# Four channel norms of part two: VectorE adds the squares, TensorE sums them into a token column

## The reference, cut to what matters

```python
def rmsnorm(x, g):
    xf = x.astype(jnp.float32)
    y = xf * lax.rsqrt(jnp.mean(xf * xf, axis=-1, keepdims=True) + EPS)
    return (y * g.astype(jnp.float32)).astype(x.dtype)

# layer 0: h = h + ab_mixer(rmsnorm(h, g0), ...)   gated delta rule and windowed attention
#          h = h + mlp(rmsnorm(h, m0))             relu squared, 1024 -> 4096 -> 1024
# layer 1: h = h + c_mixer(rmsnorm(h, g1), ...)    dense attention over 528 tokens
#          h = h + mlp(rmsnorm(h, m1))
```

## Time and profile before

| what | value |
|---|---|
| time, median of 3 runs | 3802.8 us (3795.65 to 3806.92) |
| profiled execution, first to last instruction | 3796.5 us |
| TensorE matmul busy | 2674.6 us, 70% of the span |
| VectorE busy | 2038.2 us, 54% |
| GpSimd busy | 1860.8 us, 49% |
| ScalarE busy | 802.5 us, 21% |
| mean granted TensorE clock | 0.851 |
| part two | from about 2021 us to the end |

### The profile page before, as it was taken

The page is one execution under the profiler, slowest core; times in us unless marked ns, Lnnn a source line. Parts: engine busy times, 40 slices in busy tenths (PEclk is TensorE's granted clock), DMA queues, the critical chain, the costliest instruction groups (busy, mean ns, idle before and its releaser), DMA issues.

```text
span 3796.5 us, 37057 instructions
## 1 busy us (share of the span) xinstructions
PE 2674.6 (70%) x14128; PEld 1994.0 (53%) x14128; DVE 2038.2 (54%) x4133; ACT 802.5 (21%) x1515; POOL 1860.8 (49%) x1389
## 2 busy tenths in 40 slices
PE   6521887207862277542776888888889998998999
PEld 3421444004431144211224777777789997777887
DVE  6599867888678877588443534544220103532010
ACT  2100111001110011111113322332332322443231
POOL 0166656775567756488761322222354543125463
PEclk8755999558886599776998987998999999999999
DMA  5388889897899879999991210000223332012332
GB/s 173 138 310 299 288 276 338 306 341 261 298 314 344 314 264 333 343 336 336 353 345 28 67 28 1 1 1 1 56 73 91 88 90 59 26 45 78 95 95 78
DMA packets 417970, 693.79 MB, mean 183 GB/s; under 512 B 35784, under 2 KB 280691, under 8 KB 417667
## 3 DMA queue, kind: packets, MB, share of 16 engines
q0 software_dynamic: 147456, 536.94, 39.7%
q1 hardware_dynamic: 270339, 154.50, 14.1%
HBM read 689.26 MB, written 2.10 MB: 182 GB/s over the span
## 4 chain that ended last, share of the span: by engine, by line
PE 51%; DVE 16%; POOL 12%; DMA 11%; issue 6%; ACT 3%; SPq 1%; DVEq 0%; ACTq 0%; POOLq 0%
PE PS L1601 25%; POOL ring L608 12%; DMA ring<-in_peer_v,eidx 7%; PE PS L775 7%; DMA ring<-in_peer_u,eidx 3%; DVE ring L1308 3%; PE PS L754 2%; PE PS L1502 1%; PE PS L1511 1%; PE PS L660 1%; PE PS L1508 1%; DVE W L1182 1%; PE PS L1611 1%; DVE X L1323 1%; PE PS L1623 1%
## 5 line engine op out<-in xcount | busy, mean ns | idle before, releaser
L608 POOL DMA_INDIRECT ring<-in_peer_u,eidx x512 | 630.7, 1232 | 409.1 <-DVE eidx L1285 175.9
L608 POOL DMA_INDIRECT ring<-in_peer_v,eidx x512 | 588.9, 1150 | 355.2 <-PE PS L775 215.4
L1601 PE MATMUL PS<-held_uH,GW 128*128 128x264 f32 (+1 forms) x3008 | 668.3, 316 | 35.4 <-POOL BIG_value L2128 31.3
L1308 DVE CUSTOM_DVE_ANT_0 ring<-ring,hn 128x1024 f32<-128x1024 f32 x512 | 615.7, 1224 | 117.9 <-DMA ring<-in_peer_u,eidx 110.8
L775 PE MATMUL PS<-ring,dg 128*128 128x512 f32 x1024 | 534.9, 662 | 168.7 <-DMA ring<-in_peer_v,eidx 164.4
L2114 POOL TENSOR_TENSOR GW<-held_wr,GW 128x1024 fp32r<-128x1024 f32 x178 | 428.9, 2411 | 449.5 <-ACT GW L1891 449.5
L1601 PEld LDWEIGHTS PS<-held_uH,GW 128*128 128x128 f32 x3008 | 504.2, 193 | 79.9 <-issue 34.1
L1601 PE MATMUL PS<-BIG_value,GW 128*128 128x264 f32 (+1 forms) x1504 | 448.1, 313 | 0.0
L775 PEld LDWEIGHTS PS<-ring,dg 128*128 128x128 f32 x1024 | 198.0, 208 | 460.8 <-DMA ring<-in_peer_v,eidx 281.3
L1323 DVE SCALAR_TENSOR_TENSOR X<-ring,gact,X 128x1024 f32<-128x1024 f32 x256 | 328.7, 1284 | 179.8 <-DMA ring<-in_peer_v,eidx 176.0
L1601 PE MATMUL PS<-hid,GW 128*128 128x264 f32 (+1 forms) x2304 | 368.6, 322 | 0.0
(11 more groups left out here) (465 smaller groups left out, 3581.1 us busy)
## 6 DMA issues: line engine op xcount, KB each, us to landing
held_wr<-in_w_ff SPq DMA_DIRECT2D x128, 512.0 KB, 4.1
wqr<-in_peer_wq SPq DMA_DIRECT2D x64, 512.0 KB, 8.0
held_wr<-in_w_in_ab SPq DMA_DIRECT2D x18, 512.0 KB, 3.7
ring<-in_peer_u,eidx POOLq DMA_INDIRECT x512, 6.2
ring<-in_peer_v,eidx POOLq DMA_INDIRECT x512, 6.0
BIG<-in_w_in SPq DMA_DIRECT2D x4, 1536.0 KB, 11.3
held_wr<-in_w_qkv_c SPq DMA_DIRECT2D x12, 512.0 KB, 3.9
w_out<-in_w_out SPq DMA_DIRECT2D x1, 4096.0 KB, 20.6
```

What stands on the lines that cost most here:

```text
L608: e.indirect_dma_start(out=ring[:, i % RING, :], out_offset=None, in_=rows_u if k < HK else rows_v, in_offset=bass.IndirectOffsetOnAxis(ap ...
L1308: e.tensor_tensor_reduce(row, row, hn[:, :], 1.0, 0.0, ALU.mult, ALU.add, act[:, k:k + 1]).then_inc(*n.up(e_dot))
L1601: ins = e.matmul(bank[b + a][:, 0:w], (hi, lo)[w_][:, k * P:(k + 1) * P], (x_hi, x_lo)[x_][:, c0:c0 + w], start=(first and w_ == 0 and x_ ...
```

## The change

It touches the four channel norms alone.

- VectorE adds the squares of tiles 0 to 6 into `R` (`add_square`): six adds of a full tile for each norm. The square of tile 7 stays in `sq[1]`.
- TensorE's `sums` calls for these norms go. In their place `norm` issues, behind the last gemm, short matmuls whose stationary operand is a slice of `R` and whose moving operand is one column of 1/1024 (`share`): 6 slices of 88 tokens in ALL, 4 of 128 in LATE. Each leaves the sum of its tokens as a column, token by partition. The same is done with `sq[1]`, into another bank.
- VectorE adds EPS to the first column block, and then adds the second; ScalarE takes the root, VectorE the reciprocal, all on 88 by 6 (or 128 by 4) values.
- TensorE spreads them back to rows by 6 (4) matmuls: stationary the column broadcast to 128, moving the identity. VectorE's multiply for `uT` then reads the inverse root from PSUM and not from `R`.

```diff
+    two["share"] = np.full((P, 1), 1.0 / D, f)
...
+    ALL, LATE = Span(0, 264, 2, 88), Span(META, 512, 1, P)
...
-        def norm(from_k, sp=ALL):
-            for k in range(from_k, 8):
-                sums(ones2, sq[k % 2], k == 0, k == 7, sp)
+        def norm(inverted, sp=ALL):
+            w = sp.few
+            for src, ready, at in ((R, nxt(n_acc, 6), 4), (sq[1], nxt(n_sq, 8), 5)):
+                e.wait_ge(*ready)
+                for i, c0 in enumerate(sp.cuts):
+                    ins = e.matmul(bank[at][0:w, 300 + i:301 + i], src[:, c0:c0 + w], share, start=True, stop=True)
+                ins.then_inc(*up(n_sum))
+            e.wait_ge(rinv, inverted)
+            for i in range(len(sp.cuts)):
+                ins = e.matmul(sp.row_sums(i), vec2[0:w, 98 + i:99 + i].to_broadcast([w, P]), ident2[0:w, 0:w], start=True, stop=True)
+            ins.then_inc(*up(n_sum))
             return normed()
...
             for m in range(8):
                 gemm(operands if m == 0 else [waited(o) for o in operands], h_res, sp)
-                if squares and m:
-                    sums(ones2, sq[(m - 1) % 2], m == 1, False)
...
+        def square_tile(k, sp=ALL):
+            if k >= 2:
+                e.wait_ge(n_acc, count["norm"] + max(k - 2, 1))
+            e.activation(sp.cut(sq[k % 2]), sp.cut(hT[:, k, :]), ACT.Square).then_inc(*up(n_sq))
...
-            d = sp.cut(R)
-            sqrt(e, n, d)
+            sqrt(e, n, vec2[0:sp.few, 98:98 + len(sp.cuts)])
...
+        def add_square(k, sp=ALL):
+            e.wait_ge(*nxt(n_sq, 2 if k == 1 else 1))
...
+                e.tensor_tensor(sp.cut(R), sp.cut(R), sp.cut(sq[k % 2]), ALU.add).then_inc(*up(n_acc))
...
         def norm(gcol, sp=ALL):
-            summed(8)
-            inverse((sp.two(R), sp.cut(R)), sp.pair(4), 1.0 / D)
+            summed()
+            part = lambda at: bank[at][0:sp.few, 300:300 + len(sp.cuts)]
+            few = vec2[0:sp.few, 98:98 + len(sp.cuts)]
+            e.tensor_scalar(few, part(4), EPS, None, ALU.add).then_inc(*up(dve))
+            e.wait_ge(*now(dve))
+            summed()
+            e.tensor_tensor(few, few, part(5), ALU.add).then_inc(*up(var))
+            e.wait_ge(*nxt(root))
+            e.reciprocal(few, few).then_inc(*up(rinv))
...
-                e.scalar_tensor_tensor(sp.cut(uT[:, k, :]), sp.cut(hT[:, k, :]), vec2[:, gcol + k:gcol + k + 1], sp.cut(R),
+                e.scalar_tensor_tensor(sp.two(uT[:, k, :]), sp.two(hT[:, k, :]), vec2[:, gcol + k:gcol + k + 1], sp.pair(4),
                                        ALU.mult, ALU.mult).then_inc(*up(n_u))
...
             for m in range(8):
                 b = output(units, sp)
+                if squares and m >= 2:
+                    add_square(m - 1, sp)
                 e.wait_ge(g_done, count["unit"])
```

More of the change, by code:

```diff
@@ L436, in emit, with __init__ @@
     class Span:
-        def __init__(self, c0, w, parts):
-            self.c0, self.w, self.parts = c0, w, parts
+        def __init__(self, c0, w, parts, few):
+            self.c0, self.w, self.parts, self.few = c0, w, parts, few
+            self.cuts = range(c0, c0 + w * parts, few)
             self.halves = [(c0 + w * a, w) for a in range(parts)]
@@ L456, in pair, with row_sums @@
             return PS[0:rows, b:b + self.parts, 0:self.w]
-    ALL, LATE = Span(0, 264, 2), Span(META, 512, 1)
+        def row_sums(self, i):
+            c = i * self.few
+            return PS[:, 4 + c // self.w, c % self.w:c % self.w + self.few]
+    ALL, LATE = Span(0, 264, 2, 88), Span(META, 512, 1, P)
     def row(m, width):
@@ L1630, in waited, with residual @@
             return [(hi, lo, None) for hi, lo, _ in operands]
-        def norm(from_k, sp=ALL):
-            for k in range(from_k, 8):
-                sums(ones2, sq[k % 2], k == 0, k == 7, sp)
+        def norm(inverted, sp=ALL):
[9 more added lines that the diff above has]
+            ins.then_inc(*up(n_sum))
             return normed()
-        def residual(operands, squares, sp=ALL):
+        def residual(operands, sp=ALL):
             for m in range(8):
                 gemm(operands if m == 0 else [waited(o) for o in operands], h_res, sp)
-                if squares and m:
-                    sums(ones2, sq[(m - 1) % 2], m == 1, False)
         def mlp(last):
             sp = LATE if last else ALL
-            ops = norm(7, sp)
+            ops = norm(INV_MLP1 if last else INV_MLP0, sp)
             for half in range(2):
@@ L1650, in mlp @@
                 hops = [(r(hid[:, 0, m, :]), r(hid[:, 1, m, :]), nxt(lo_g)) for m in range(16)]
-                residual([hops[0:8], hops[8:16]], half and not last, sp)
+                residual([hops[0:8], hops[8:16]], sp)
         e.wait_ge(t_hT, 2 * NB)
@@ L1657, in second_tensor @@
         e.transpose(bank[6][:, 0:97], vr2[0:97, :], ident2[0:97, 0:97]).then_inc(*up(s_vecp))
-        ops = norm(0)
+        ops = norm(INV_NORM0)
         e.wait_ge(n_w16, 2)
@@ L1730, in second_tensor @@
         yops = [(r(uH[:, k, :]), r(uL[:, k, :]), nxt(lo_g if (k < 4) == (k % 2 == 1) else lo_v)) for k in range(8)]
-        residual([yops], True)
+        residual([yops])
         mlp(False)
-        ops = norm(7)
+        ops = norm(INV_C)
         def rope(m):
@@ L1797, in second_tensor @@
         yops = [(r(uH[:, h, :]), r(uL[:, h, :]), nxt(lo_g)) for h in range(8)]
[L1798 to L1802, removed]
+        residual([yops], LATE)
         mlp(True)
@@ L1882, in second_scalar @@
         up, now, nxt = n.up, n.now, n.next
-        count = {"split": 0, "unit": 0, "out": 0, "sq": 0}
+        count = {"split": 0, "unit": 0, "out": 0, "sq": 0, "norm": 0}
         limit = [BEFORE_DELTA]
@@ L2345, in mlp @@
                 lows[0] += 16
-                residual(2, sp)
+                residual(2, half and not last, sp)
         lows = [0]
@@ L2353, in second_vector @@
         e.wait_ge(*now(dve))
+        for k in range(1, 7):
+            add_square(k)
         norm(0)
@@ L2449, in second_vector @@
         lows[0] += 4
-        residual(1)
+        nxt(n_sq, 17)
+        residual(1, True)
         lows[0] += 4
@@ L2511, in second_vector @@
         lows[0] += 8
-        residual(1, LATE)
+        nxt(n_sq, 10)
+        residual(1, True, LATE)
         lows[0] += 4
```

19 lines of the change are left out of this document (16 added, 3 removed).

## The result

The changed kernel took 3776.2 us in the median of 20 runs (3749.2 to 3802.4), the kernel before 3801.5 on the same chip (20 runs): ratio 0.9931, interval 0.9916 to 0.9947, 20 to 32 us off. The forecast was 25 us off, to 3778. The profiled execution took 3777.2 us with a span of 3775.4; before, the span was 3796.5.

The account below looks back on a forecast made before the run. The prediction took TensorE, in part two nearly all its gemms, to bound the kernel. Its terms, 15.8 + 5.0 + 3.0 + 2.0 - 0.4 = 25.4 us off, put the median at 3778 us, range 3768 to 3788.

Parts of the forecast that it names:

- own signs: Last square to first multiply was to take near 3.6, 3.6 and 2.9 us in norms MLP0, C and MLP1.
- rival A: Norm chains: granted clock falls in the pause, short matmuls double (7.8 us), full gemms slow (6); 11.6 off, 3791; chance 0.11.
- Term 1: Three residuals feeding norms: six channel sums each, 0.89 or 0.86 us, no longer hold up the next gemm; 15.8 us off.
- Term 1's cover: VectorE's adds of squares, 0.7 to 2.2 us, fit inside the shortest gemm, 5.8 us, so nobody waits.
- Terms 2 and 3: Chains from last square to first multiply: 2.5 us off each in norms MLP0 and C, 3.0 in MLP1.
- Term 4: Norm AB, adds on the path and short matmuls at half pace: first multiply 2.0 us sooner, between 1 and 5.
- Term 5: VectorE's multiply reading the inverse root from PSUM costs 0.1 us a norm, 0.4 in all.
- Rivals B and C: B (0.05): something else held the gemm, 9.6 us off; C (0.02): short matmuls don't overlap weight loads, 3812 or 3832 us.
- The sum: All gains less the PSUM cost: 15.8 + 5.0 + 3.0 + 2.0 - 0.4 = 25.4 us off, bounds 22.4 to 30.2.

Follow-up runs that it names:

- Fillers and wide slices together: Changed kernel plus unread matmuls in TensorE's norm-chain pauses and slices streaming their one column 64 times; ratio to the kernel before 0.9903, repeated 0.9915.
- fillers alone: Changed kernel plus float32 matmuls that nothing reads in TensorE's norm-chain pauses, slices still of one column; ratio to the kernel before 0.9897.
- wide slices alone: Changed kernel with every slice's matmul streaming its one column 64 times, pauses not filled; ratio to the kernel before 0.9929.

## Why the prediction was right

It was right in its time, and right in the way it said for 15.5 of the first pair's 26 us and, nearly, for norm AB's 2.4. For the three other chains it was not: of its own signs, 3.6, 3.6 and 2.9 us did not come (5.31, 4.74 and 4.00), and rival A's, a granted clock of 0.5 in the chain, did. By its own steps:

**Term 1**, 15.8 us: 15.5 measured, in every profile of the changed kernel, and given by the adds alone. Two full sums or the column make no difference to it. The missing 0.3 is mostly mixer AB's projection, where a sum cost 0.84 us from one residual add to the next (6.71 against 5.87) and not 0.89.

**Term 1's cover**: the adds take 0.69 to 0.71 us, and no gemm waits, even with three times as many. The place where an add could take 2.2 us did not arise: the prediction put the adds beside GpSimd's splits, and they end ahead of them. The shortest gemm is 5.6 us and not 5.8, which changes nothing.

**Terms 2 and 3**, 8.0 us: mis-sized, 4.25 measured (0.84 + 1.42 + 1.99). The mechanism was right and the steps at full clock were right: slices 1.10 (1.3 taken, bounds 1.0 to 1.55), small steps with their hand-overs 0.77 (0.65), spreads 1.57 where the clock stayed (1.55). What failed is the pace of a record, 0.114 us by rows at full clock, taken for spreads that ran at a granted clock of 0.50: the changed kernel's spreads took 2.70 and 2.86 us, MLP1's 2.02 (1.09 taken). Fillers and wide slices together gave 3.66 and 3.67 for the forecast's 3.6 and, 0.3 above it, 3.2 for 2.9.

**Rival A**, 0.11, had this mechanism, "the clock falls during the pause". Its first half came, at the price of 3.5 us (what the kernel with both means gives back: 1.65, 1.07 and 0.80) and not 7.8: the eighth tile's slices had run before the clock fell, wholly in C and MLP1 and in part in MLP0. Its second half, a low clock in full gemms that costs time, did not: the first of them ran at 0.50 until 3149, and the clock was back (0.95 over 3149 to 3152) while VectorE still set the pace. In MLP0 it is 12.74 us from the first multiply to the unbroken row of gemms in both kernels. Its reason against, "now no pause is over 3 us", was true and no protection.

**Term 4**, 2.0 us: 2.4 in the first pair. Of the 0.4, nearly half is rounding (2038.16 less 2036.0 is 2.2), and the rest comes from slices and spreads that were quicker than taken. The adds ended 6.65 us behind the start of the first square (6.5 taken), the 24 records at half clock took 3.68 (4.1), the spreads 2.86 (3.1). Against the other two profiles of before it is up to 3.0. The term counts the adds and the column together, rightly: the adds alone give 15.3 us, the column alone 18.9, both 14.1.

**Term 5**, 0.4 us of cost: none; two multiplies took 1.44 (1.45 before). (TensorE's share in part two of the kernel before is nine tenths or more in eight of its 18 whole slices and eight tenths in the other ten, not nine tenths in most; no term hangs on it.)

**Rivals B and C**: the next gemm came at once, so nothing stood behind the sums; short matmuls are 0.09 us apart in the slices (1.10 for twelve), not 0.30. C's price at 0.36 us a record is 2.2 a norm by its own sum, not 2.4.

**The sum** was near partly by luck: 25.4 forecast, 22.2 explained (15.5 + 4.25 + 2.4), and in the first pair 3.9 from the mixers that two executions of the same code may differ in by more. The timed ratios put the gain at 20 to 32, 20 to 40 and 27 to 48 us; the last lies above 22.2. Part two took 1774.9, 1782.4 and 1783.7 us in the three profiles of before and 1748.9, 1747.8 and 1747.6 in those of the changed kernel, 32 us apart in the mean, of which the AB mixer is some 9. Whether the changed kernel meets the mixer's good pattern more often in timed runs (654 to 655 in four of five profiles with its norm AB, against 657.8 at best in three of before), or part one has a share, stays open: the profiles are too few, and timed runs carry no trace.

## What to carry to other kernels

Sums that stood between full gemms were worth all their time here (15.5 of 15.8 us), and an engine that is idle through each gemm took them at no cost; count the gaps and believe that number. A chain shortened by turning wide vector work into short matmuls must be priced at half of TensorE's clock, unless rows show that the clock holds there. With more columns for the short matmuls and the pauses filled it held in all nine late chains of three profiles, where it fell in all nine of the changed kernel's. In norm AB, where TensorE stood at 0.50, the short matmuls without the adds made the norm longer. And before a rest of a few microseconds in untouched code is put down to a change, profile the old kernel again.

## What was not expected of the hardware

- Twelve matmul records of one moving column (1.10 us) let the granted clock fall to 0.51 soon after, and the same twelve with 64 columns (1.15 us) did not, with the same pauses.
- In norm MLP1 the clock fell with fillers alone (0.55 over 3397 to 3398) and with wide slices alone (chain 4.01 us), and held with both (3.20), but also with neither in the kernel with the column alone (3.31).
- The AB mixer, 654 to 667 us, differs by 8.9 us between three executions of one program and by up to 12.6 between kernels with the same instructions in it; where the traces were laid side by side, a burst of matmuls met 1.00 in the one and 0.50 in the other, and 7 us were lost.
- Twelve short matmul records of one column between two gemms cost 0.95 us, more than four full ones of 264 columns (0.84 to 0.89).
